# Thirty-two more rows of an input projection as three one-pass products, with low parts made by accumulating transfers

## The reference, cut to what matters

```
xn   = rmsnorm(x)
proj = xn @ w_in                       # 2048 x 5120: sb q,k,v | ssm u | diff q,k,v
y    = concat[ stick_breaking(q,k,v), s5_mixer(u), differential(q,k,v) ]
h    = x + y @ w_out
out  = rmsnorm(h + hierarchical_moe(rmsnorm(h)))
```

## Time and profile before

| | |
|---|---|
| Timed runs | 1421.82, 1420.91, 1422.08 us; median 1421.82 |
| Profiled execution | span 1421.0 us from first to last instruction, 0.8 us below the median |
| Busy time | TensorE 1355.8, weight loads 766.4, VectorE 537.2, ScalarE 347.3, GpSimd 228.6 us |
| Granted TensorE clock | mean 0.988 |
| Bytes | 471.76 MB in 71540 packets, mean 332 GB/s |

### The profile page before, as it was taken

How to read it: one execution, slowest core, us unless ns; L and a number is a source line. 1 busy time by engine, 2 the same in 40 slices (tenths; PEclk the granted TensorE clock), 3 DMA queues, 4 the chain that set the end, 5 groups by cost and what they waited for, 6 DMA issues and landing times.

```text
span 1421.0 us, 19044 instructions
## 1 busy us (share of the span) xinstructions
PE 1355.8 (95%) x7236; PEld 766.4 (54%) x7236; DVE 537.2 (38%) x1017; ACT 347.3 (24%) x623; POOL 228.6 (16%) x205
## 2 busy tenths in 40 slices
PE   7999999999999999998998999999999999898987
PEld 7884898987786345444433533544544543443533
DVE  6999420544425233233313323223323331331315
ACT  1121378566571111110210110111111121111003
POOL 2002756687881000000000000000000000000000
PEclk9999999999999999999999999999999999999999
DMA  8433543434475999999999999959999999999993
GB/s 214 178 119 119 208 178 119 155 142 161 140 292 235 384 428 428 427 428 427 428 429 428 429 428 428 428 224 429 428 428 428 428 428 428 429 428 428 428 425 138
DMA packets 71540, 471.76 MB, mean 332 GB/s; under 512 B 17329, under 2 KB 17410, under 8 KB 46274
## 3 DMA queue, kind: packets, MB, share of 16 engines
q1 hardware_dynamic: 70834, 469.75, 80.5%
q10 hardware_dynamic: 528, 1.05, 0.2%
q0 software_dynamic: 128, 0.26, 0.1%
HBM read 468.95 MB, written 2.10 MB: 331 GB/s over the span
## 4 chain that ended last, share of the span: by engine, by line
PE 62%; DMA 19%; DVE 2%; ACT 1%; issue 1%; POOL 1%; DVEq 0%; POOLq 0%; SPq 0%; ACTq 0%
PE ps L1932 24%; DMA ring<-in_expert_w_dram 18%; PE ps L1950 12%; PE ps L1590 11%; PE ps L1910 5%; PE ps L1940 3%; PE ps L1968 2%; PE ps L1969 1%; DMA reg_e<-in_expert_w_dram 1%; POOL w_lo L570 1%; PE ps L1922 1%; PE ps L1857 0%; DVE reg_x L1518 0%; DVE reg_y L1134 0%; PE ps L1764 0%
## 5 line engine op out<-in xcount | busy, mean ns | idle before, releaser
L1950 PE MATMUL ps<-ring,reg_y 128*64 128x512 f32 x1056 | 241.8, 611 | 14.1 <-issue 7.4
L570 POOL TENSOR_TENSOR w_lo<-ring,w_hi 128x512 fp32r<-128x512 f32 x152 | 199.8, 1347 | 72.5 <-ACT w_hi L632 71.3
L1950 PEld LDWEIGHTS ps<-ring,reg_y 128*64 128x64 f32 x1056 | 76.0, 140 | 153.0 <-issue 148.4
L1407 DVE TENSOR_TENSOR y_lo_t<-ps,y_hi_t 64x512 fp32r<-64x512 f32 x128 | 88.2, 689 | 171.6 <-ACT y_hi_t L866 169.6
L866 ACT ACTIVATE y_hi_t<-ps 64x512 fp32r<-64x512 f32 x132 | 78.0, 591 | 279.9 <-PE ps L1950 278.3
L1415 DVE TENSOR_TENSOR reg_x<-ps,reg_x 128x512 f32<-128x512 f32 x128 | 82.2, 684 | 152.3 <-PE ps L1969 152.3
L1932 PE MATMUL ps<-reg_e,reg_s 128*64 128x512 f32 x528 | 119.4, 594 | 10.5 <-POOLq L595 10.5
L1932 PE MATMUL ps<-ring,reg_s 128*64 128x512 f32 x528 | 120.0, 596 | 7.2 <-POOLq L595 6.7
L1396 DVE TENSOR_SCALAR reg_y<-ps,lamv 128x512 f32<-128x512 f32 x33 | 24.8, 751 | 269.0 <-PE ps L1932 269.0
L1932 PE MATMUL ps<-ring,reg_y 128*64 128x512 f32 x528 | 119.9, 596 | 5.5 <-POOLq L595 5.0
L1932 PE MATMUL ps<-reg_e,reg_y 128*64 128x512 f32 x528 | 119.4, 594 | 3.8 <-POOLq L595 2.3
(11 more groups left out here) (405 smaller groups left out, 1759.9 us busy)
## 6 DMA issues: line engine op xcount, KB each, us to landing
ring<-in_expert_w_dram SPq DMA_DIRECT2D x128, 2048.0 KB, 20.1
reg_e<-in_expert_w_dram SPq DMA_DIRECT2D x64, 2048.0 KB, 20.5
ring<-in_w_in_dram SPq DMA_DIRECT2D x19, 2048.0 KB, 7.6
ring<-in_w_out_dram SPq DMA_DIRECT2D x8, 2048.0 KB, 7.9
reg_x<-in_x_dram SPq DMA_DIRECT2D x4, 1024.0 KB, 8.3
ring<-in_w_in_dram SPq DMA_DIRECT2D x2, 1024.0 KB, 7.3
out_dram<-reg_x SPq DMA_DIRECT2D x3, 512.0 KB, 2.7
reg_e<-in_ssm_w_glu_dram ACTq DMA_DIRECT2D x1, 1024.0 KB, 8.6
```

The source lines that it names most:

```text
L570: G.tensor_tensor(w_lo[:, i % BUFS, :], unit(u % SLOTS_A)[:, c, :], w_hi[:, i % BUFS, :], ALU.subtract).then_inc(row_lo, 1)
L1407: V.tensor_tensor(y_lo_t[64 * q:64 * q + 64, w], psb[3 + k // 2][64 * (k % 2):64 * (k % 2) + 64, :], y_hi_t[64 * q:64 * q + 64, w], ALU.su ...
L1950: last = M(psb[3 + i // 2][64 * (i % 2):64 * (i % 2) + 64, :], hT[:, 2 * half + f, :], unit2(s)[:, f, 512 * i:512 * i + 512], start=half = ...
```

## The change

R0, the first row with the old split, stays 72; a new R1 = 40 is the first one-pass row. Rows 40 to 71 are early rows:

- ACT writes both the high part and, with scale -1, its negative into the low part's buffer (two copies a row).
- GpSimd issues a transfer that adds the row's weights from HBM onto that buffer, so it then holds weights minus high part (`early_lows`, `accum_op`). The row is so read twice from HBM, once into the ring, once here.
- TensorE waits for that transfer (early_in, one semaphore for each of AHEAD = 8 buffers) in place of row_lo.
- Four of the eight buffers are w_hi and w_lo, four more lie in reg_y and reg_s, unused then. ACT may run seven rows ahead.
- x_low follows rows 24 to 39 in place of 56 to 71. GpSimd issues the transfers of rows 40 to 43 between the last four x_low, the others behind them.
- S_STEP and Y_STEP are spaced by three parts from part 17 on; Y_STEP[-1] is 38 instead of 36, and P_GLU and all behind it are two parts later.
- ACT's copies of early rows stand ahead of each decay; evac(2) and evac(3) are placed before decay(5) and decay(7).
- SP's waits and its order are the same.

```diff
-R0 = 72
-X_ORDER = [(R0 + i) % DC for i in range(DC)]
+R1, R0, AHEAD = 40, 72, 8
+X_ORDER = [(R1 + i) % DC for i in range(DC)]
 P_BT = 4
-S_STEP = [9] + [15 + 27 * k // 10 for k in range(ST // 2 - 1)]
-Y_STEP = [17 + (27 * k + 9) // 10 for k in range(ST // 2)]
+S_STEP = [9, 15, 17, 20, 23, 26, 29, 32]
+Y_STEP = [17, 20, 23, 26, 29, 32, 35, 38]
...
+        early_hi = nc.alloc_sbuf_tensor_at("early_hi", [P, 4, 512], R, offset=reg_y_at + 4 * 2048)
+        early_lo = nc.alloc_sbuf_tensor_at("early_lo", [P, 2, 512], R, offset=reg_y_at)
...
+        early_lo2 = nc.alloc_sbuf_tensor_at("early_lo2", [P, 2, 512], R, offset=reg_s_at + 4 * 2048)
...
+        def row_parts(i):
+            j = (i - R1) % AHEAD if i < R0 else i % BUFS
+            if j < BUFS:
+                return w_hi[:, j, :], w_lo[:, j, :]
+            return early_hi[:, j - BUFS, :], early_lo[:, j - BUFS, :] if j < BUFS + 2 else early_lo2[:, j - BUFS - 2, :]
...
             def x_low(chunks):
                 for c in chunks:
-                    g.wait_ge(row_used, R0 - DC + X_ORDER.index(c) + 1)
+                    g.wait_ge(row_used, R1 - DC + X_ORDER.index(c) + 1)
                     G.tensor_tensor(act_lo[:, c, :], act_x[:, c, :], act_hi[:, c, :], ALU.subtract).then_inc(x_lo, 1)
+            def early_lows(rows):
+                for i in rows:
+                    n_, cc = i // DC, i % DC
+                    c0 = BLOCKS[n_][2]
+                    g.wait_ge(row_hi, i - R1 + 1)
+                    g.dma_start(row_parts(i)[1], w_in_u[:, cc, c0:c0 + 512], accum_op=ALU.add).then_inc(early_in[(i - R1) % AHEAD], 16)
 
             g.wait_ge(x_hi, 1)
             x_low(X_ORDER[0:12])
-            lows(R0)
-            x_low(X_ORDER[12:])
+            for k in range(4):
+                early_lows((R1 + k,))
+                x_low(X_ORDER[12 + k:13 + k])
+            early_lows(range(R1 + 4, R0))
             lows(ROWS)
...
-                while row[0] < min(done + BUFS, ROWS):
+                while row[0] < min(done + (BUFS if row[0] >= R0 else AHEAD - 1), ROWS):
...
+                    if i < R0:
+                        if i - R1 >= AHEAD:
+                            a.wait_ge(row_used, i - AHEAD + 1)
+                        A.activation(hi, w, cp)
+                        A.activation(lo, w, cp, scale=-1.0).then_inc(row_hi, 1)
+                    else:
                         a.wait_ge(row_used, i - BUFS + 1)
+                        A.activation(hi, w, cp).then_inc(row_hi, 1)
...
-            for p in range(2, 5):
+            for p in range(2, ST // 2):
+                if p == 5:
+                    evac(2)
+                if p == 7:
+                    evac(3)
+                highs(rows_done(Y_STEP[p - 2]) - 4)
                 decay(p)
-            evac(2)
-            for p in range(5, ST // 2):
-                decay(p)
-            evac(3)
...
-                pe.wait_ge(row_lo, i - R0 + 1)
-                return w_hi[:, i % BUFS, :], w_lo[:, i % BUFS, :]
+                if i < R0:
+                    pe.wait_ge(early_in[(i - R1) % AHEAD], 16 * ((i - R1) // AHEAD + 1))
+                else:
+                    pe.wait_ge(row_lo, i - R0 + 1)
+                return row_parts(i)
```

More of the change, by code:

```diff
@@ L248, in build @@
         row_used = sem("row_used")
+        early_in = [sem(f"early_in{j}") for j in range(AHEAD)]
         y_hi = sem("y_hi")
@@ L568, in lows @@
                     u, c = i // 8, i % 8
-                    g.wait_ge(row_hi, i - R0 + 1)
+                    g.wait_ge(row_hi, i - R1 + 1)
                     G.tensor_tensor(w_lo[:, i % BUFS, :], unit(u % SLOTS_A)[:, c, :], w_hi[:, i % BUFS, :], ALU.subtract).then_inc(row_lo, 1)
@@ L620, in _ @@
             A.activation(rms_b, at[3][:, T:2 * T], cp).then_inc(rms_row, 1)
-            row = [R0]
+            row = [R1]
             def highs(done):
-                while row[0] < min(done + BUFS, ROWS):
+                while row[0] < min(done + (BUFS if row[0] >= R0 else AHEAD - 1), ROWS):
                     i = row[0]
@@ L629, in highs @@
                         a.wait_ge(ring_in[u % SLOTS_A], 16 * (u // SLOTS_A + 1))
-                    if i - R0 >= BUFS:
+                    w = unit(u % SLOTS_A)[:, c, :]
+                    hi, lo = row_parts(i)
+                    if i < R0:
[4 more added lines that the diff above has]
+                    else:
                         a.wait_ge(row_used, i - BUFS + 1)
-                    A.activation(w_hi[:, i % BUFS, :], unit(u % SLOTS_A)[:, c, :], cp).then_inc(row_hi, 1)
+                        A.activation(hi, w, cp).then_inc(row_hi, 1)
                     row[0] += 1
@@ L1628, in project @@
                 for cc in (2 * (part % 8), 2 * (part % 8) + 1):
-                    if 16 * n_ + cc < R0:
+                    if 16 * n_ + cc < R1:
                         native_row(n_, cc, banks).then_inc(row_used, 1)
@@ L1632, in project @@
                     w = next_row()
-                    if 16 * n_ + cc < R0 + DC:
+                    if 16 * n_ + cc < R1 + DC:
                         pe.wait_ge(x_lo, X_ORDER.index(cc) + 1)
```

## The result

| | before | after |
|---|---|---|
| median (range) | 1421.49 us (1420.91 to 1422.08, 4 runs) | 1437.69 us (1434.73 to 1438.19, 4 runs) |
| ratio after / before, 95% interval | | 1.0111 [1.0098, 1.0124] |
| span of the profiled execution | 1421.0 us | 1436.2 us |
| mean granted clock | | 0.984 |

The change makes the kernel 1.1% slower, beyond the upper end of the range. In the profile after, the one-pass and three-product code is L1618, the native rows are L1647, the ring loads L494, x_low L588 and the accumulating transfers L596.

What follows compares the result with a forecast made beforehand. TensorE, busy for 95% of 1421.0 us, was taken as the bound. Terms of -2.9 (ahead at row 72), +1.1 (clock) and +1.0 (tail) gave -0.8 on the span, hence a median of 1421.0 us; 8-in-10 range 1412 to 1431.

Steps and rivals of the forecast that it cites:

- Start: Before row 40: its transfer issues at 92.9 us and lands at about 98.5, leaving TensorE empty for 7.6 us.
- Loss up to row 48: Rows 40 to 47: late transfers move row 48's start from 109.06 to 114.9 us, losing 5.8 us.
- The ring turn: Ring units of early rows: 12.8 us from issue to first row, just covered by 13.1; left out of the sum.
- the rival: Ring units 7 and 8: turn of 18.9 us against 15.2 and 13.1 of cover, 9.5 lost, 1430.5 us; chance 0.12.
- Price on the engines: Accumulating transfers of early rows: 1.34 us of the DMA engines per row, twice the 0.67 of a copy.
- The rival of the engines: Early rows: DMA engines become the bound, 16.1 us per unit where TensorE took 16.9; 1426 us, chance 0.09.
- Clock: Rows 40 and 41: TensorE falls to the 1.2 GHz level behind the 7.6 us gap, costing 1.1 us (0 to 3.4).
- Tail: df_sums(0) moves from row 148 to 152: one y_high more on ACT, costing 1.0 us (0 to 2).
- VectorE's chain: Pairs of states: lengthened by 7.2 us, last state at 154 us, wanted past 160, so covered.
- the saving of 11.2: TensorE's rows 40 to 71: one-pass instead of native saves 5.1 + 6.1 = 11.2 us if rows are ready in time.
- the three signs named for being wrong: First one-pass row before 94 or after 102; transfer under 3 or over 7 us; waits for early rows after row 48.

Runs made afterwards that it cites:

- Early release: Changed kernel, but SP issues units 7 to 10 once ACT has copied the slot's rows, not once TensorE has used them: 1427.56 us, ratio 1.0045.
- eight of eight rows: Changed kernel with ring slots released after ScalarE's copies, tail on its old rows, x_low interleaved with transfers, and S_STEP, Y_STEP of the kernel before: 1420.06 us.
- interleaved: Changed kernel with GpSimd's order changed: four x_low, then each transfer of rows 40 to 47 followed by one more x_low: 1434.25 us, ratio 1.0088.
- four of eight rows: Changed kernel with each unit's first four rows native, slots released early, x_low reordered, tail and steps as in the kernel before: 1414.98 us, ratio 0.9958.

## Why the prediction was wrong, step by step

- **Start: right.** 7.6 us of empty TensorE were forecast, 8.87 measured; issue of row 40's transfer at 92.9, measured 92.5 after the shift of 1.65; x_low 1.3 us, measured 1.16; VectorE's pair over 12 us, measured 13.5. The extra 1.3 us are the transfer's: 7.4 us from its issue to the product, 5.6 forecast.
- **Loss up to row 48: 5.8 forecast, 9.1 measured.** Of the difference 2.6 us are the clock, which the prediction has as a term of its own: of the 10.2 us at 0.50 TensorE works in 5.2, and loses half of these; the part spent waiting costs nothing. Another 1.3 are the longer wait, less 0.6 forecast for row 44, which did not have to wait.
- **The ring turn: this step failed.** "From then to its first row: load 7.6, two copies 1.2, transfer 4.0 = 12.8 us. [...] It just covers. I leave it out of the sum". For row 56 the turn was 18.4 us, from the issue at 117.87 to the product at 136.28: load 12.8, copies and GpSimd 1.4, transfer 4.2. The rows of the unit in between took 15.4 us (the 15.2 that the rival names ahead of unit 7; the 13.1 is the cover ahead of unit 8), so TensorE waited 2.99 us; row 57's transfer, beside the next ring load, took 7.7 us from issue to product, which made 3.43 more. What was mis-sized is the ring load, which the transfers beside it lengthened by 5.2 us; the landing of 4.0 held for row 56. Early release, which shortens only the turn, gave 10.1 us back: these 6.4 us and 3.4 of clock. The rival had a turn of 18.9 us and a time of 1430.5, with landings of 7.4 us and a delay of 2.7: the right chain, and a sum that came close partly by luck. A cover of 0.3 us ahead of unit 8, and of 2.4 ahead of unit 7, under durations that the change itself lengthens should have been the likeliest case and not one at 0.12.
- **Price on the engines: 1.34 us a row forecast, measured 1.5** (3.5% of 1436.2 us is 50 us for 4736 packets; the 4096 of these rows take 48.6 us of it, with a median of 178 ns and a mean of 190). The Trainium skill's rule ("Collectives: The Full Stack", The bandwidth ceiling), about half of a copy's rate, agrees with the runs: 99 ns for a plain packet of the same queue, 1.8 times, and 84 ns for the ring's, 2.1 times. The rival of the engines (16.1 us a unit) had the price nearly right, but it was not the bound of the changed kernel, since early release ran the same bytes 10 us faster. It is the bound behind it, as far as the windows tell: with the turn short and the start covered, eight of eight rows keep the engines' share at 1.06 to 1.09 from 100 to 150 us and save nothing.
- **Clock: 1.1 forecast, 6.0 measured,** because the low level came twice and lasted 10.2 us each time, not 3. TensorE worked in 5.2 us of the first stretch and 6.8 of the second, and lost half of that.
- **Tail: 1.0 forecast (0 to 2), 6.3 measured.** I priced one y_high more on ScalarE. What was late next was VectorE's chain behind df_sums; I had not followed it. The steps alone made 1428.3 us of the kernel before, 7.7 us more in the median; in the profiled execution 6.4 us are lost here.
- **VectorE's chain: covered only because the rows were late.** Its last state was forecast at 154 us. In the kernel without transfers TensorE waits for it up to 159.42.
- **Not foreseen:** 6.6 us given back in the last stage. At the place of the long wait, 5.4 us before, there are 2.1 and 1.0 now, and 5.6 us of work at 0.50 behind it are gone: 2.2 and 2.8 us, a matter of the program's place and not of the change. The other 1.6 stay open.

In the sum the saving of 11.2 is right. Against it stand 8.9 for row 40, 6.0 of clock, 6.4 of waits for the ring turn, 6.3 of tail and 1.65 of start: 29.3, so +18 at the first expert load. It was +21.8; of the 3.7 left 2.3 are small waits for low parts in the rows, and the rest stays open. Two of the three signs named for being wrong are there: transfers over 7 us to landing, and waits for early rows after row 48.

## What to carry to other kernels

When a transfer is put between a load and its use, add up the turn (release, load, copies, transfer) with the durations that it will have beside the new traffic, and treat a cover within a few microseconds as a wait. Then add up the engines' time per unit beside TensorE's: a shorter turn does not help past that. If either is short, mix rows that need no transfer with those that do. With early release, the interleaved or mixed order on GpSimd and the old steps, four of eight rows gave 6 us and eight of eight 1 us, which is within the noise. Move a schedule's later steps only if a profile shows that they wait, and check each variant's last stage for a wait that has nothing to do with the edit before crediting the edit with it.

## What the runs showed of the hardware

- An accumulating 2 KB packet took 176 to 178 ns in most cases, a plain one of the same queue 99. GpSimd needed 0.86 us in the median to issue an accumulating transfer and 0.53 a plain one.
- Ring loads of 2 MB were copied 7.8 and 7.9 us after issue without transfers beside them, 10.4 to 12.8 us with plain ones and 12.8 to 16.9 with accumulating ones. Accumulating transfers landed 4.1 to 12.2 us after issue (median 7.7).
- With 32 accumulating transfers and early release the engines' share from 100 to 150 us was 1.06 to 1.10, and TensorE waited for low parts; with 20 it was 0.92, and TensorE did not.
- TensorE's clock was at 0.50 for 10.2 us twice: from within a wait of 8.9 us on, and from 1.2 us after a wait of 3.0 us on, with a wait of 3.4 us inside. Behind waits of 5.2 to 5.8 us near the end it was there for 6.8 us, from within the wait on.
- A wait of TensorE on nothing that the profile names, near the end, was absent, 2.1 to 2.5 or 5.2 to 5.8 us; a packet of the queue "instruction" had started 2.8 to 2.9 us before the end of each of the longest. The same rows had 1.5 us at its place, and 5.5 with 32 matmuls added some 1355 us before.
